# Products of the residual rows and the norms' rows moved from VectorE to GpSimd, a quarter at a time

## What is computed

```python
def rms_norm(x, w):
    y = xf * lax.rsqrt(jnp.mean(xf * xf, axis=-1, keepdims=True) + EPS)
    return (y * w.astype(jnp.float32)).astype(x.dtype)
...
    x = x + m
    x = x + squared_relu_mlp(rms_norm(x, norm_ffn[i]), ffn_w1[i], ffn_w2[i])
```

## Time and profile before

| | |
|---|---|
| median of three runs | 2332.12 us (2330.89 to 2332.69) |
| the profiled execution, its own time | 2332.59 us |
| its span, first to last instruction | 2330.8 us |
| TensorE busy | 2309.6 us (99%) |
| VectorE busy | 1585.4 us (68%) |
| ScalarE busy | 1215.7 us (52%) |
| GpSimd busy | 85.1 us (4%) |
| granted TensorE clock, mean over the span | 0.998 |

### The profile page before, as it was taken

How to read it: one execution, slowest core, us unless ns; L and a number is a source line. 1 busy time by engine, 2 the same in 40 slices (tenths; PEclk the granted TensorE clock), 3 DMA queues, 4 the chain that set the end, 5 groups by cost and what they waited for, 6 DMA issues and landing times.

```text
span 2330.8 us, 31488 instructions
## 1 busy us (share of the span) xinstructions
PE 2309.6 (99%) x12562; PEld 1945.2 (83%) x12562; DVE 1585.4 (68%) x1684; ACT 1215.7 (52%) x1361; POOL 85.1 (4%) x136
## 2 busy tenths in 40 slices
PE   9999999999999999999999999999999999999998
PEld 8788888888888788887788888888888888888887
DVE  7667666876666765686576567887756677877565
ACT  6545435464456644564454355544644655546444
POOL 0000030200000000000000000000000000000000
PEclk9999999999999999999999999999999999999999
DMA  7554654644444355545454444445454544454543
GB/s 276 190 178 174 247 200 188 201 167 191 180 182 152 126 201 210 198 177 187 178 203 181 189 182 178 152 168 211 168 200 178 212 185 159 163 195 179 200 168 143
DMA packets 71850, 432.18 MB, mean 185 GB/s; under 512 B 11648, under 2 KB 11968, under 8 KB 26432
## 3 DMA queue, kind: packets, MB, share of 16 engines
q1 hardware_dynamic: 59760, 400.87, 45.1%
q0 software_dynamic: 11984, 29.82, 4.4%
HBM read 428.66 MB, written 6.16 MB: 187 GB/s over the span
## 4 chain that ended last, share of the span: by engine, by line
PE 91%; DVE 5%; ACT 2%; DMA 1%; issue 1%; POOL 0%; SPq 0%; DVEq 0%; ACTq 0%
PE pair L839 21%; PE pair L842 10%; PE acc L810 10%; PE acc L811 10%; PE acc L812 10%; PE pair L810 6%; PE pair L812 5%; PE pair L811 5%; PE pair L851 5%; PE pair L852 2%; DVE w_lo L1997 1%; DVE work L2394 1%; PE pair L985 1%; PE pair L887 1%; PE acc L1258 1%
## 5 line engine op out<-in xcount | busy, mean ns | idle before, releaser
L1997 DVE TENSOR_TENSOR w_lo<-raw,w_hi 128x2048 fp32r<-128x2048 f32 (+1 forms) x402 | 866.0, 2175 | 103.8 <-ACT w_hi L1367 100.0
L1367 ACT ACTIVATE w_hi<-raw 128x2048 fp32r<-128x2048 f32 (+1 forms) x402 | 717.0, 1805 | 59.5 <-PE acc L812 46.6
L839 PE MATMUL pair<-act,w_hi 128*128 128x512 f32 x1920 | 602.5, 395 | 0.0
L842 PEld LDWEIGHTS pair<-act,w_lo 128*128 128x128 f32 x1920 | 360.7, 188 | 84.8
L842 PE MATMUL pair<-act,w_lo 128*128 128x256 f32 x1920 | 377.2, 278 | 0.0
L810 PE MATMUL acc<-w_hi,hid 128*128 128x512 f32 x848 | 334.0, 394 | 0.0
L811 PE MATMUL acc<-w_lo,hid 128*128 128x512 f32 x848 | 330.4, 390 | 0.0
L812 PE MATMUL acc<-w_hi,hid 128*128 128x512 f32 x848 | 330.3, 389 | 0.0
L1525 ACT ACTIVATE gate<-pair 128x512 f32<-128x512 f32 x104 | 62.2, 598 | 458.9 <-PE pair L842 436.4
L839 PEld LDWEIGHTS pair<-act,w_hi 128*128 128x128 f32 x1920 | 295.4, 189 | 3.6
L2204 DVE TENSOR_TENSOR gate<-pair,gate 128x512 f32<-128x512 f32 x104 | 71.7, 690 | 256.3 <-ACT gate L1525 255.8
(11 more groups left out here) (297 smaller groups left out, 2870.4 us busy)
## 6 DMA issues: line engine op xcount, KB each, us to landing
raw<-weights SPq DMA_DIRECT2D x354, 1024.0 KB, 6.7
raw<-weights SPq DMA_DIRECT2D x52, 512.0 KB, 4.0
work<-bias_scratch POOLq DMA_DIRECT2D x32, 192.0 KB, 2.8
val<-gains POOLq DMA_DIRECT2D x11, 512.0 KB, 4.0
bias_scratch<-bias_rows POOLq DMA_DIRECT2D x4, 1024.0 KB, 19.9
hid<-u_rows POOLq DMA_DIRECT2D x20, 142.0 KB, 3.3
work<-ret_gn_w POOLq DMA_DIRECT2D x8, 256.0 KB, 5.4
work<-ret_gn_b POOLq DMA_DIRECT2D x8, 256.0 KB, 6.6
```

The source lines that it names most:

```text
L839: mm(tiles(o[:, 512 * n:512 * n + 512]), h[:, k, n * P:(n + 1) * P], both[:, :, k, :], start=k == 0, stop=False)
L842: last = mm(o[:, 512 * n:512 * n + SEQ], l[:, k, n * P:(n + 1) * P], both[:, 0, k, :], start=False, stop=k == KT - 1)
L1367: run(w_hi[slot][:, part], raw[slot][:, part], ACT.Copy).then_inc(hi_done, 1)
L1997: tt(w_lo[slot][:, part], raw[slot][:, part], w_hi[slot][:, part].bitcast(F32), ALU.subtract).then_inc(lo_done, 1)
```

## The change

The gain's products of norms 0 to 10 leave VectorE. `gain_row` on GpSimd, after it has fetched the row, waits for it, and then makes the four products of that norm, each after its quarter's `x_ready` (after the second one of each quarter in norm 7, which is that of `BY_ROW`), and signals `by_gain`. ScalarE's scaled copies wait for `by_gain`, one for each quarter. The last norm's products stay on VectorE.

```diff
-            def gain_row(chunks):
+            def gain_row(chunks, row=False):
 
                 S.c += chunks
                 pool.wait_ge(act_lo_done, S.c - 1)
-                fetch(val[:, S.c % 2, :], row_of(rows["gains"][S.due("gains") - 1, :]), gain_in)
+                gain, norms = val[:, S.c % 2, :], S.due("gains")
+                fetch(gain, row_of(rows["gains"][norms - 1, :]), gain_in)
                 S.c += 4
+                pool.wait_ge(gain_in, 16 * norms)
+                for a in range(2):
+                    for n in range(2):
+                        pool.wait_ge(x_ready, S.due("x_ready", 2 if row else 1))
+                        nc.gpsimd.tensor_tensor(xs[:, a, wide(n)], (BY_ROW if row else x)[:, a, wide(n)], gain[:, wide(n)],
+                                                ALU.mult).then_inc(by_gain, 1)
...
                 link(root(a))
                 for n in range(2):
+                    act.wait_ge(by_gain, S.due("by_gain"))
                     run(dst[:, a, wide(n)], xs[:, a, wide(n)], ACT.Copy, scale=rstd[:, a:a + 1]).then_inc(done, 1)
...
-                        if (a, n) == (0, 0):
-                            if row:
+                        if (a, n) == (0, 0) and row:
                                 dve.wait_ge(row_in, 16 * S.due("row_norms"))
-                            dve.wait_ge(gain_in, 16 * S.due("gain_in"))
                         if row:
                             tt(BY_ROW[:, a, wide(n)], x[:, a, wide(n)], ROW[:, wide(n)], ALU.mult).then_inc(x_ready, 1)
                             dve.wait_ge(x_ready, S.due("x_ready"))
-                            by_row(a, n, gain, BY_ROW)
-                        else:
-                            by_row(a, n, gain, x)
```

More of the change, by code:

```diff
@@ L390, in build_program @@
         x_ready = sem("x_ready")
+        by_gain = sem("by_gain")
         ss_ready = sem("ss_ready")
@@ L762, in _ @@
                 bias_tile(1)
-                gain_row(FFN2_CHUNKS if layer else FFN1_CHUNKS)
+                gain_row(FFN2_CHUNKS if layer else FFN1_CHUNKS, layer == 0)
                 for j in range(2, 8):
@@ L2152, in norm @@
                     split_piece(S.u, 0)
-                gain = val[:, S.c % 2, :]
                 def lows(a):
```

## The result

The changed kernel takes 2335.97 us (median of 18 runs, 2332.52 to 2339.35) against 2332.64 for the kernel before (18 runs, 2330.89 to 2333.78): the ratio is 1.0014, with a 95% interval of 1.0008 to 1.0020, or 3.3 us (1.9 to 4.7). Forecast was +1.8 us and, most likely, a difference within 0.2%. Its profiled execution took 2336.76 us, with a span of 2335.0. Its runs spread over 6.8 us, those of before over 2.9.

A forecast was written before the change was run, and what follows sets the result against it. TensorE, busy 99% of the span, was taken to bound the kernel, with some 5.6 us of waits at norms. Terms 1.1 - 0.4 + 0.46 + 0.46 + 0.15 = +1.8 us gave 2333.9 us, range 2330.5 to 2340.5.

The forecast's parts named there:

- The product beside the square: VectorE's norm 1 product (388.04 to 388.73), wholly beside ScalarE's sum of squares; removing it moves `inverse_rms` by nothing.
- The second rival: Single-column instructions do not stand behind GpSimd, so `inverse_rms` mostly stays in place: -3.3 us, 2328.8; chance 0.12.
- P = 1.15: P is the time in us of one 128x512 gain product on GpSimd, taken near the upper of two halves.
- the halves' range: Estimates for P from halving double-width GpSimd products: half of 1.78 is 0.89, half of 2.42 is 1.21.
- the first rival: Slower: GpSimd's product is long where `inverse_rms` stands behind it; from P = 1.33 the sum passes 4.7 us; chance 0.22.
- d = 0.41 us: How far `inverse_rms` moves back behind GpSimd's product: d = P + 0.05 - 0.79.
- 0.22 us in each of norms 0, 1, 6, 8, 10: TensorE, not waiting there before, stands for 0.41 - 0.19 us per norm; five norms give +1.1 us.
- The slack of 0.19 us in norm 1: Time from the copies' end at 390.76 to the first transpose needing the second copy, at 390.95.
- Norms 3 and 5, -0.2 each: TensorE's 0.45 us wait for `lows`: these come 0.61 earlier and 0.41 later, the turn's stand inside that wait; -0.4 together.
- Norms 2 and 4, +0.23 each: Back-to-back residual sums give GpSimd two products in a row; `inverse_rms` starts at 495.38 against 495.15; +0.46 together.
- Norm 7, +0.15: `lows` gain some 0.26 us at the 1.6 wait; second-half copies, already waited for, come later by 0.41 less that.
- Norm 9, +0.46: Two products in a row in each half, where TensorE already waits for copies (1.2 and 0.40 us): +0.23 per half.

The follow-up runs named there:

- the other form: Changed kernel, `inverse_rms`'s first instruction taking one column as tensor, the other as per-partition scalar: 2329.84 us against 2332.49 before; same form without GpSimd products: 2333.03 against 2332.36.
- `inverse_rms` late: Kernel before, all products on VectorE, with three linked one-column instructions ahead of `inverse_rms` in norms 0 to 10: 2341.13 us against 2332.36, ratio 1.0038.
- the half: Changed kernel with only products (0, 0) and (1, 0) on GpSimd, the others on VectorE: 2328.73 us against 2332.49 before; repeated, 2329.09 against 2332.26.

## Why the prediction was right, point by point

- **The product beside the square is worth nothing; those ahead of `lows` and of a residual sum are in the path.** Right. With the hold gone, norms 3 and 5 gain 0.3 to 0.5, norms 2 and 4 0.2 to 0.4, and norms 6, 8 and 10 next to nothing (-0.08 to 0.09). A small part was not seen: without a product in front of it `inverse_rms` starts 0.87 us after the residual sum, not 0.79.
- **Two instructions with both inputs in SBUF do not share, and residual sums and `lows` go on.** Right. The Trainium skill's "SBUF — State Buffer", in its summary of rules, makes no exception for small instructions, and the trace agrees: an instruction on one column stood for 0.37 us on top of its 0.16. The second rival had bet against that and is out, but its arithmetic had a point: -3.3 us without the hold, and -2.7 measured once the hold was taken away by the other form.
- **P = 1.15 and a start 0.05 us behind the residual sum.** Measured: 1.29 and 0.09. Both ends of the halves' range (0.89 and 1.21) were too low: a product of half the width costs more than half of 1.78. A part at its start that was hidden in those rows and is open here would explain it; no run separates such a part. The estimate of 1.12 us by the Trainium skill's "GPSIMD Engine Reference", section 3.1, was too low as well, by 0.17; the page's 4497 ns is for an addition of two tensors, and the trace has a multiplication. The point of the first rival, 1.33, was near but not reached.
- **d = 0.41 us.** The copies come 0.45 us later. The product ends 1.38 us after the residual sum, by which d would be 0.59; but a held instruction ended only 0.02 us after it, where an instruction that is issued then would run for 0.16. That gave back 0.14 of the 0.18 that P and the start had taken: d came out nearly right by luck.
- **0.22 us in each of norms 0, 1, 6, 8, 10.** This is the term that was mis-sized: 0.35 to 0.42 measured. The slack of 0.19 us in norm 1 was not there. TensorE turns 0.15 us after a copy's end, and I had counted from the copy's end itself: 390.76 + 0.15 is 390.91, against 390.95 for the transpose that needs it, a slack of 0.04, so that nearly all of d went to TensorE: 0.45 - 0.04 = 0.41. The trace of before had this distance, in norm 2, where TensorE waited for the first copy (ended at 495.77 + 0.72 = 496.49). ScalarE's row and TensorE's there:

```profile
495.77 1.34 ACT L1446 ACTIVATE work<-work,small 128x512 f32<-128x512 f32 x2
```

```profile
496.64 1.18 PE L887 MATMUL pair<-ident,work 128*128 128x128 f32 x8 [0.38 <-ACT work L1446]
```

  Over five norms this is 0.9 us of the 1.5 that the median was above the forecast.
- **Norms 3 and 5, -0.2 each.** Measured -0.03 to -0.09; the wait of 0.45 us, of which 0.25 was to stay, went whole, but the stand at the turn came on top of it and not inside it.
- **Norms 2 and 4, +0.23 each.** Measured 0.32 to 0.37: two products in a row count P twice.
- **Norm 7, +0.15.** Measured 0.25 and 0.41. TensorE's wait of 1.6 us there shrank by 0.1 and not by 0.26, and that for the second half's copies grew from 0.2 to 0.6.
- **Norm 9, +0.46.** Not seen apart from the fall of the clock in either profile (1.24 and 2.60 with it).
- **ScalarE's waits for `by_gain` cost nothing; the fetches behind the products cost nothing.** Right for the first, as no such wait is in the trace. No wait for the group norm's rows appeared either.
- **The sum, +1.8 us, 2333.9.** Measured +3.3 (1.9 to 4.7) and 2335.97, inside the range of 2330.5 to 2340.5, and within 0.2%. What the sum left out is the falls of TensorE's clock. Both profiles of the changed kernel have one in norm 9, and the profile of before that the sum started from has one too, in a stage that the sum did not look at. How much of the difference they make is not settled: the norm terms of the second profile, norm 1 taken as 0.4 and norm 9 left out, make 2.9 us (with 0.38 for norm 0), and norm 9 with its falls and the falls of before come on top with either sign. The mean clock of each execution says a little more. Of the 29 executions of the changed kernel the three at 1.000 took 2332.2 to 2332.9 us and the six at 0.997 2336.3 to 2339.4. Of the 92 of before that are listed with their clock none is at 0.997, and the 38 at 0.998 lie 0.6 us above the 14 at 1.000 (means of 2332.5 and 2331.9). So the changed kernel's longer executions are on the whole those with the lower clock. Whether the falls cost that time, or come with longer stands that cost it, these numbers do not tell.

## What to carry to other kernels

In this case a VectorE instruction with two tensor inputs in SBUF stood until a running GpSimd product ended, even one on a single column (0.53 us instead of 0.16), and it showed as busy time, not as a wait: look for short instructions whose duration has grown. Before work goes to GpSimd, list what VectorE issues in the next 1.3 us and give that list a form with one tensor input (PSUM or a scalar for the other), or place on GpSimd only what ends before such an instruction is due. When slack is read from a trace, count it from when the waiting engine can start (here 0.15 us after ScalarE's end), not from the end of the work.

## What the runs showed that I had not expected

- A scalar for each partition, read from SBUF, does not count as a second input: 0.21 us beside a running product, against 0.53 for the form with two tensor inputs.
- The stand is not a fixed price: an instruction held by the product ended 0.02 us after it, though it is 0.16 long alone.
- TensorE's granted clock falls from 2.4 to 1.2 GHz for some 3 to 7 us after stands in norms 2, 7 or 9 or in the convolution stage. Nine of the twelve profiles have such a fall, with and without the change: both of the changed kernel and both of before, that of norm 9 back on VectorE, that of `inverse_rms` late (three falls), those of the scalar form with all of GpSimd's products and with none, and one of two of the half. Norms with a fall are 0.9 to 2.6 us dearer in the table, with what else changed in them. Stands of equal length went with and without one (in norm 2 one of 1.9 us with a fall, in the second profile of before, and one of 2.3 us without, in the first of the changed kernel), so what tips it stays open. It is one source of the scatter of a kernel's runs, and not the only one: the eleven executions with (0, 1) and (1, 1) on GpSimd spread over 4.3 us with mean clocks of 0.998 and 0.999 alone.
